# Two layers and a product-key expert block in fp32: the first two query panels of the second layer computed token tile by token tile, and the wait for the sub-keys moved

## The chip, the cores and the metric

The kernel runs on one core of a Trainium2 chip. The metric is the device time of one execution in microseconds (us), the median of three runs. Everything is computed to fp32 accuracy: each large product is three passes of TensorE over operands split in a high and a low part (high·high, high·low, low·high). All times of one instruction come from one profiled execution.

## The reference, cut to what matters

Two transformer blocks run one after the other on 256 tokens of width 1024. The second block has two layers (called layer 1 and layer 2 here, `l = 0` and `l = 1` in the code). Each layer is a mixing part, a layer norm, a product-key expert part, and another layer norm:

```python
y = jnp.concatenate([mix, mo], axis=-1) @ w_out[l]
x = _layer_norm(DN_ALPHA * x + y, ln_mix_g[l], ln_mix_b[l])
f = _peer(x, peer_w_q[l], peer_sub_keys[l], peer_u[l], peer_v[l])
x = _layer_norm(DN_ALPHA * x + f, ln_ffn_g[l], ln_ffn_b[l])

def _peer(x, w_q, sub_keys, u, v):
    xt = x.reshape(T, D)                                      # 256 x 1024
    q = (xt @ w_q).reshape(T, PEER_HEADS, 2, PEER_HALF)       # 8 heads, 2 sides, 128
    s = jnp.einsum('thpe,pne->thpn', q, sub_keys)             # 128 sub-keys for each side
    top_s, top_i = lax.top_k(s, PEER_TOPK)                    # 16 of each side
    ...                                                       # 16 of the 256 sums, softmax, experts
```

The change lies where `x` has just been normed and `q` is computed, in both layers.

## The kernel before, in words

**Weights.** All weights come as one stream of panels of 128 x 2048 fp32 (1 MB). SyncE loads panel `i` into `RAW[i % 4]`; ScalarE copies it rounded to `HI` (function `hi`, L467); VectorE, or GpSimd in a stretch of each layer, subtracts to get the low part `LO` (L982, L1577). There are four slots. TensorE waits for the low part (`lo_ready`) and counts used panels in `hp_used`; ScalarE may fill a `HI` slot again once the panel four earlier is used; SyncE may load a `RAW` slot again once its low part is made. The order on each engine is the order in which the Python code issues it; nothing is scheduled later.

**The norm.** The output product of the mixing ends in four PSUM banks: two token tiles of 128 tokens, two column halves. VectorE adds the residual (`add_mixed`, L1400), takes statistics, and norms one tile at a time (`norm_tile`, L1207 to L1216; the last step is L1215, which signals `x_tile`). TensorE then turns that tile, eight 128 x 128 transposes (`tile_transposes`, L1615) into `M[0]`, `M[1]` for tile 0 and `M[2]`, `M[3]` for tile 1; ScalarE copies out the high part `XH` (L487), VectorE the low part `XL` (L1005, signal `xl_ready`), each in two groups of four 128-column blocks. While tile 1 is normed, TensorE computes a panel of the memory keys in layer 1 (`mem_panel(3)`), and in layer 2 issues 20 products whose result is never read (`warm(20, M[2])`, L1597).

**The queries.** Eight panels follow from `w0` on, one for each head: `half(w0 + u, "cc")` computes 2 x 128 query columns for all 256 tokens, with the weight block stationary and the 256 turned tokens moving, 2 halves x 8 blocks x 3 passes = 48 matmuls (L1620 to L1622). ScalarE copies each result to `QP` (L827). `head_scores(h)` multiplies head `h` by the sub-keys `SK` (four fp32 matmuls, eight TensorE instructions, L2193), ScalarE copies the scores to `SC` (L816), and VectorE looks for the best 16 (`best16`, L1221 to L1231). The sub-keys come by a DMA that ScalarE issues after both tiles are normed, behind a store of `X` to DRAM (L819, L820). TensorE waits for `keys_loaded` ahead of the first query panel (L2196).

**Behind them.** From `d0 = w0 + 8` on come the dense expert panels. The first 32 are products alone, and in their course VectorE finishes the selection that started with the eight heads.

Of the kernel before, what the change touches and what calls it, by code (L numbers as in the profile page):

```python
# [12 lines left out]
ACT = mybir.ActivationFunctionType  # L13
AX = mybir.AxisListType

P = 128
LOW = 128
TOK = 256
TT = TOK // P
# [112 lines left out]
def build(nc, stream, x_in, mem_in, const_in, par_in, lb_in, par2_in, wg2_in, mask_in, lev_in, rows_in, sk_in, diag_in, out):  # L132
    ctx = ExitStack()
    with ctx:
        sems = {}

        def sem(name):
            if name not in sems:
                sems[name] = ctx.enter_context(nc.semaphore(name))
            return sems[name]  # L140
# [5 lines left out]
        def at(name, shape, dt=F32, off=None):  # L146
            size = int(np.prod(shape[1:])) * (2 if dt == BF16 else 4)
            o = cursor[0] if off is None else off
            if off is None:
                cursor[0] += (size + 63) // 64 * 64  # L150
            assert o + size <= end, (name, o + size, end)
            return nc.alloc_sbuf_tensor_at(name, list(shape), dt, offset=o)
# [78 lines left out]
        def cst(name):  # L231
            a, b = CONST[name]
            return CST[:, a:b]
# [5 lines left out]
        def flat(t):  # L239
            return t.rearrange("p a b -> p (a b)")  # L240
# [53 lines left out]
        topk0 = x0 + TABLE_AT * slot  # L294
        cursor[0] = topk0
        TFX = at("tfx", [P, 2, TT * PH, TOPK, TOPK], BF16, off=topk0)
        QP = at("qp", [P, 2 * PH, TOK])
        CD2 = at("cd2", [P, PH, CANDS], off=cursor[0])
        EQ = at("eq", [P, TT * PH, TOPK, TOPK], BF16, off=cursor[0] + 8192)
        SC = at("sc", [P, TT, 2 * PH, KEYS])  # L300
# [40 lines left out]
        PS = [ctx.enter_context(nc.psum_tensor(f"lin{i}", [P, 512], F32)) for i in range(4)]  # L341
        M = [ctx.enter_context(nc.psum_tensor(f"m{i}", [P, 512], F32)) for i in range(4)]
# [5 lines left out]
        bank_free = [sem(f"bank_free{i}") for i in range(4)]  # L348
# [13 lines left out]
        def evicted(eng, i, it=0):  # L362

            eng.wait_ge(bank_free[i % 4], reads_before(i) + 1 + it)
# [93 lines left out]
        def _(act):  # L458
# [63 lines left out]
            for l in range(DEPTH):  # L522
# [21 lines left out]
                for u in range(N_IN):  # L544
                    hi_to(h0 + u + 4)
                    i = h0 + u
# [7 lines left out]
                    if u == 4:  # L554
# [3 lines left out]
                        ins = act.activation(flat(VA[:]), b[:, 256:512], ACT.Copy)  # L558
# [68 lines left out]
            for l in range(DEPTH):  # L627
# [16 lines left out]
                else:  # L644
                    xh_tile(6, 1)
                    for u in range(N_SHARED):
                        hi_to(HP_SHARED + u + 4)
                        i = HP_SHARED + u
# [174 lines left out]
                for u in range(N_WQ):  # L823
                    hi_to(w0 + u + 4)
                    i = w0 + u
                    act.wait_ge(hp_used, i + 1)
                    act.activation(flat(QP[:, 2 * u:2 * u + 2, :]), PS[i % 4][:], ACT.Copy).then_inc(bank_free[i % 4], 1)  # L827
                    if u >= 1:
                        head_scores(u - 1)
                head_scores(PH - 1)  # L830
# [762 lines left out]
        def _(pe):  # L1593
            def warm(n, bank):

                for _ in range(n):
                    pe.matmul(bank[:, 0:256], cst("ident"), CST[:, 0:256], start=True, stop=True)  # L1597
# [12 lines left out]
            def tile_transposes(inst, tt):  # L1610

                pe.wait_ge(sem("x_tile"), 2 * (inst - 5) + tt + 1)
                for g in range(2):
                    for k in range(4):
                        ins = pe.transpose(M[2 * tt + g][:, P * k:P * k + P], X[:, tt, P * (4 * g + k):P * (4 * g + k) + P], cst("ident"))  # L1615
                    ins.then_inc(sem("t_done"), 1)
# [12 lines left out]
            def half(i, modes, it=0, hh=XH, hl=XL, k0=0, first=True, last=True, between=lambda c: None, inst=None, tiled=None):  # L1629

                hp_wait(i, it, first)

                def operand(start, k):

                    if inst is not None and start and k % 2 == 0:
                        pe.wait_ge(sem("xl_ready"), 4 * inst + k // 2 + 1)
                    if tiled is not None and start and k % 4 == 0:
                        pe.wait_ge(sem("xl_ready"), 4 * tiled + 2 + k // 4 + 1)

                s, b = i % SLOTS, PS[i % 4]  # L1640
                wh, wl = (t.rearrange("p (k n) -> p k n", k=KT) for t in (HI[s][:], low_part(i)))
                if modes == "rr":
                    for tt in range(TT):
                        if tt == 1:
                            between(0)
                        for k in range(KT):
                            operand(tt == 0, k)
                            ins = three(b[:, 256 * tt:256 * tt + 256], hh[:, k0 + k, P * tt:P * tt + P], hl[:, k0 + k, P * tt:P * tt + P],
                                        wh[:, k, :], wl[:, k, :], first and k == 0 and (last or tt == 0), last and k == KT - 1, skip_group_check=not (first and last))
                else:  # L1650
                    for c, mode in enumerate(modes):
                        if c == 1:
                            between(0)
                        n = slice(P * c, P * c + P)
                        if mode == "c":
                            for k in range(KT):
                                operand(c == 0, k)
                                ins = three(b[:, 256 * c:256 * c + 256], wh[:, k, n], wl[:, k, n], hh[:, k, :], hl[:, k, :], k == 0, k == KT - 1)
                        else:
                            for tt in range(TT):  # L1660
                                for k in range(KT):
                                    ins = three(b[:, 256 * c + P * tt:256 * c + P * tt + P], hh[:, k, P * tt:P * tt + P], hl[:, k, P * tt:P * tt + P],
                                                wh[:, k, n], wl[:, k, n], k == 0, k == KT - 1)
                ins.then_inc(hp_used, 1)
                between(1)
# [266 lines left out]
            for l in range(DEPTH):  # L1932
# [247 lines left out]
                if l == 0:  # L2180
                    mem_panel(3)
                else:
                    warm(20, M[2])
                tile_transposes(5 + 2 * l, 1)
                def head_scores(h):

                    evicted(pe, w0 + h)
                    if h >= 4:
                        pe.wait_ge(sem("keysc_ready"), PH * l + h - 3)
                    for tt in range(TT):  # L2190
                        for side in range(2):
                            c = 256 * tt + P * side
                            ins = pe.matmul(M[h % 4][:, c:c + P], QP[:, 2 * h + side, P * tt:P * tt + P], SK[:, side, :], start=True, stop=True)  # L2193
                    ins.then_inc(sem("keysc_done"), 1)

                pe.wait_ge(sem("keys_loaded"), 16 * (l + 1))  # L2196
                for u in range(N_WQ):
                    half(w0 + u, "cc", tiled=5 + 2 * l if u == 0 else None)
                    if u >= 1:
                        head_scores(u - 1)  # L2200
                head_scores(PH - 1)
                d0 = w0 + N_WQ
# [269 lines left out]
```

## Time and profile before

| what | value |
|---|---|
| median of 3 runs | 2642.83 us (2639.48 to 2645.89) |
| profiled execution, own time | 2644.11 us |
| its span in the trace | 2642.3 us |
| TensorE matmul busy | 2580.5 us, 98% of the span |
| VectorE, ScalarE, GpSimd busy | 64%, 50%, 6% |
| DMA | 520.14 MB, mean 197 GB/s |
| mean granted TensorE clock | 0.995 of full speed |

The execution's own time is 1.8 us longer than the span of its records. TensorE is busy nearly always, so what counts is where it stands still, where it does work that nobody needs, and where it runs at the lower of its two clocks. Such places are found in the list of waits, in the chain of work that ended last (each row is a start, a duration, and what was done) and in the windows.

### The profile page before, as it was taken

Reading aid. Unit: us, or ns where it says so; the run is one execution under the profiler, and the core shown is the slowest. Engines: PE = TensorE matmul, PEld = TensorE weight load, DVE = VectorE, ACT = ScalarE, POOL = GpSimd, SP = SyncE. Lnnn points to the kernel's source line nnn. Section 1 sums busy time; section 2 is a strip of 40 time slices with the busy share of each in tenths; the row PEclk is TensorE's granted clock in tenths of the full one; section 3 lists DMA queues with packets and bytes.
Section 4 is the critical chain, followed back from the end, with each engine's and each line's share of the span. In section 5 each row is a group of like instructions: output and inputs, shape, how many; then the busy total and the mean of one; then the engine's idle time right before and its main releaser. Section 6 shows DMA issues by size and latency. Waiting matters only on the chain.

```text
span 2642.3 us, 45690 instructions
## 1 busy us (share of the span) xinstructions
PE 2580.5 (98%) x18680; PEld 2352.4 (89%) x18680; DVE 1689.2 (64%) x2677; ACT 1323.8 (50%) x1585; POOL 163.1 (6%) x74
## 2 busy tenths in 40 slices
PE   8999999999999999999999999988999999999998
PEld 7889898798888999999999888978999999999887
DVE  5766457664456999655555666475999655555666
ACT  4455343454364679544444444443679544444443
POOL 0000000000003500000000000002600000000000
PEclk9999999999999999999999999999999999999999
DMA  6245552355526456766656675524456756666672
GB/s 244 94 180 190 193 211 94 135 203 196 195 90 219 145 203 228 287 217 212 221 210 222 231 275 183 205 80 152 154 195 236 285 210 222 214 215 217 230 273 106
DMA packets 75007, 520.14 MB, mean 197 GB/s; under 512 B 8352, under 2 KB 8624, under 8 KB 18928
## 3 DMA queue, kind: packets, MB, share of 16 engines
q1 hardware_dynamic: 58592, 424.70, 44.8%
q0 software_dynamic: 10208, 43.45, 4.7%
q10 hardware_dynamic: 6064, 49.97, 4.6%
q8 instruction: 103, 1.69, 0.3%
q14 instruction: 40, 0.33, 0.0%
HBM read 478.25 MB, written 39.85 MB: 196 GB/s over the span
## 4 chain that ended last, share of the span: by engine, by line
PE 88%; DVE 9%; ACT 2%; issue 1%; DMA 1%; ACTq 0%; DVEq 0%
PE lin L1620 17%; PE lin L1622 17%; PE lin L1621 17%; PE m L1620 9%; PE m L1621 9%; PE m L1622 9%; PE m L2214 4%; DVE lo L982 1%; PE m L1754 1%; PE lin L1816 1%; PE m L1597 1%; PE m L1775 1%; PE m L2193 0%; ACT hi L467 0%; PE m L2096 0%
## 5 line engine op out<-in xcount | busy, mean ns | idle before, releaser
L982 DVE TENSOR_TENSOR lo<-raw,hi 128x2048 fp32r<-128x2048 f32 x351 | 802.4, 2291 | 635.8 <-ACT hi L467 634.8
L467 ACT ACTIVATE hi<-raw 128x2048 fp32r<-128x2048 f32 x403 | 770.0, 1913 | 456.9 <-PE m L1622 331.7
L1620 PE MATMUL lin<-xh,hi 128*128 128x256 f32 x3376 | 954.4, 283 | 16.2 <-DMA sk<-keys 9.3
L1622 PE MATMUL lin<-xh,lo 128*128 128x256 f32 x3376 | 935.8, 277 | 0.0
L1621 PE MATMUL lin<-xl,hi 128*128 128x256 f32 x3376 | 935.8, 277 | 0.0
L1620 PEld LDWEIGHTS lin<-xh,hi 128*128 128x128 f32 x3376 | 636.4, 189 | 24.2 <-DMA sk<-keys 9.7
L1621 PEld LDWEIGHTS lin<-xl,hi 128*128 128x128 f32 x3376 | 636.6, 189 | 3.7 <-issue 1.0
L1622 PEld LDWEIGHTS lin<-xh,lo 128*128 128x128 f32 x3376 | 636.1, 188 | 0.0
L1620 PE MATMUL m<-hi,ah 128*128 128x512 f32 x1024 | 398.8, 389 | 0.0
L1621 PE MATMUL m<-lo,ah 128*128 128x512 f32 x1024 | 398.8, 389 | 0.0
L1622 PE MATMUL m<-hi,al 128*128 128x512 f32 x1024 | 398.6, 389 | 0.0
L841 ACT ACTIVATE h<-lin 128x512 f32<-128x512 f32 x128 | 76.2, 595 | 318.0 <-PE lin L1622 295.1
L1622 PEld LDWEIGHTS m<-hi,al 128*128 128x128 f32 x1024 | 192.2, 188 | 40.4
L1620 PEld LDWEIGHTS m<-hi,ah 128*128 128x128 f32 x1024 | 192.2, 188 | 38.3 <-DVE al L1493 0.8
L1621 PEld LDWEIGHTS m<-lo,ah 128*128 128x128 f32 x1024 | 192.2, 188 | 37.6
L1577 POOL TENSOR_TENSOR lo<-raw,hi 128x2048 fp32r<-128x2048 f32 x27 | 124.2, 4605 | 251.1 <-DVE lo L982 169.2
L2214 PE MATMUL m<-ob,oa 128*128 128x128 f32 x1024 | 135.2, 275 | 0.3 <-ACT ob L853 0.3
L2214 PEld LDWEIGHTS m<-ob,oa 128*128 128x128 f32 x1024 | 124.3, 191 | 1.5 <-issue 0.8
L1620 PE MATMUL lin<-hi,xh 128*128 128x256 f32 (+2 forms) x336 | 112.4, 334 | 4.7 <-DVE xl L997 2.0
L1583 POOL DMA_DIRECT2D g<-gate_table x32 | 28.3, 886 | 1328.3 <-DVE h L1488 971.8
L1621 PE MATMUL lin<-lo,xh 128*128 128x256 f32 (+2 forms) x336 | 109.6, 326 | 0.0
L1622 PE MATMUL lin<-hi,xl 128*128 128x256 f32 (+2 forms) x336 | 109.5, 326 | 0.0
(351 smaller groups left out, 2764.9 us busy)
## 6 DMA issues: line engine op xcount, KB each, us to landing
raw<-stream SPq DMA_DIRECT2D x403, 1024.0 KB, 4.8
gate_table<-stg ACTq DMA_DIRECT2D x16, 2048.0 KB, 10.9
g<-gate_table POOLq DMA_DIRECT2D x32, 1024.0 KB, 8.3
rows<-rows ACTq DMA_DIRECT2D x4, 1024.0 KB, 7.6
memh<-mem_turned_scratch POOLq DMA_DIRECT2D x3, 1024.0 KB, 5.0
meml<-mem_turned_scratch POOLq DMA_DIRECT2D x3, 1024.0 KB, 8.2
dg<-taps ACTq DMA_DIRECT2D x2, 1152.0 KB, 9.4
x_scratch<-x ACTq DMA_DIRECT2D x2, 1024.0 KB, 4.2
```

The costliest lines, as they stand in the source:

```text
L467: act.activation(HI[i % SLOTS][:], RAW[:, i % SLOTS, :], ACT.Copy).then_inc(hi_ready, 1)
L841: act.activation(H[:, s % AHEAD, :], PS[s % 4][:], ACT.Gelu).then_inc(sem("ge_ready"), 1)
L982: dve.tensor_tensor(low_part(i), RAW[:, i % SLOTS, :], HI[i % SLOTS][:].bitcast(F32), ALU.subtract).then_inc(lo_ready, 1)
L1577: pool.tensor_tensor(low_part(i), RAW[:, i % SLOTS, :], HI[i % SLOTS][:].bitcast(F32), ALU.subtract).then_inc(lo_ready, 1)
L1583: pool.dma_start(G[c % 2][:].rearrange("p g b t -> p g (b t)"), tab[l][:, :, GB * STORE * c:GB * STORE * c + GB * STORE].rearrange("g a x ...
L1597: pe.matmul(bank[:, 0:256], cst("ident"), CST[:, 0:256], start=True, stop=True)
L1620: pe.matmul(out_, ah, bh, start=first, stop=False, **kw)
L1621: pe.matmul(out_, ah, bl, start=False, stop=False, **kw)
L1622: return pe.matmul(out_, al, bh, start=False, stop=last, **kw)
L1754: last[j] = pe.matmul(to[:, 64 * tt:64 * tt + 64].rearrange("p (b m) -> p b m", m=m), KS[o, d, t], halves(QS[o, d, t], m)[:, :, 1 - d, :], ...
L1775: last[j] = pe.matmul(halves(M[3][o, c + P * tt:c + P * tt + P], m)[:, :, 1 - d, :], VR[:, tt, 64 * h:64 * h + 64], sc[:, 64 * tt:64 * tt ...
L2214: ins = pe.matmul(M[k % 4][:, KEYS * t:KEYS * t + KEYS], oa[:, t, :], ob[:, t, :], start=True, stop=True)
```

## The change

1. In layer 2 the 20 unread products are gone. In their place TensorE computes the tile 0 part of the query panels `w0` and `w0 + 1` (`row_half`, a function that was there already: the turned tokens are stationary, the 256 weight columns move, 24 matmuls for each tile of a panel). After the transposes of tile 1 come the tile 1 parts.
2. These two results stand token by column and not column by token, so ScalarE copies them to a new buffer `QTOK` (over the place of `QP[:, 0:4]`), TensorE turns them with eight transposes in the middle of panel `w0 + 2` (`queries_turned`), and ScalarE copies them to `QP`. The scores of head 0 and head 1 then both follow behind panel `w0 + 2`.
3. In both layers the wait for `keys_loaded` stands in `head_scores(0)` and no longer ahead of panel `w0`.

```diff
+        QTOK = at("qtok", [P, 2, TT, 256], off=topk0)
...
                 for u in range(N_WQ):
                     hi_to(w0 + u + 4)
                     i = w0 + u
+                    if l > 0 and u == 2:
+                        for j in range(2):
+                            act.wait_ge(sem("queries_turned"), j + 1)
+                            act.activation(flat(QP[:, 2 * j:2 * j + 2, :]), M[j][:], ACT.Copy).then_inc(sem("queries_ready"), 1)
                     act.wait_ge(hp_used, i + 1)
+                    if l > 0 and u < 2:
+                        act.activation(QTOK[:, u].rearrange("p t c -> p (t c)"), PS[i % 4][:], ACT.Copy).then_inc(bank_free[i % 4], 1)
+                        continue
                     act.activation(flat(QP[:, 2 * u:2 * u + 2, :]), PS[i % 4][:], ACT.Copy).then_inc(bank_free[i % 4], 1)
+                    if l > 0 and u == 2:
+                        head_scores(0)
                     if u >= 1:
                         head_scores(u - 1)
...
                 if l == 0:
                     mem_panel(3)
                 else:
-                    warm(20, M[2])
+                    row_half(w0, 5 + 2 * l, 0)
+                    row_half(w0 + 1, 5 + 2 * l, 0)
                 tile_transposes(5 + 2 * l, 1)
+                if l > 0:
+                    row_half(w0, 5 + 2 * l, 1)
+                    row_half(w0 + 1, 5 + 2 * l, 1)
+
+                def queries_turned(c):
+                    if c == 0:
+                        for u in range(2):
+                            evicted(pe, w0 + u)
+                            for side in range(2):
+                                for tt in range(TT):
+                                    ins = pe.transpose(M[u][:, 256 * side + P * tt:256 * side + P * tt + P],
+                                                       QTOK[:, u, tt, P * side:P * side + P], cst("ident"))
+                            ins.then_inc(sem("queries_turned"), 1)
+
                 def head_scores(h):
 
-                    evicted(pe, w0 + h)
+                    if h == 0:
+                        pe.wait_ge(sem("keys_loaded"), 16 * (l + 1))
+                    if l > 0 and h < 2:
+                        pe.wait_ge(sem("queries_ready"), h + 1)
+                    else:
+                        evicted(pe, w0 + h)
...
-                pe.wait_ge(sem("keys_loaded"), 16 * (l + 1))
                 for u in range(N_WQ):
-                    half(w0 + u, "cc", tiled=5 + 2 * l if u == 0 else None)
-                    if u >= 1:
+                    if l == 0:
+                        half(w0 + u, "cc", tiled=5 if u == 0 else None)
+                    elif u == 2:
+                        half(w0 + u, "cc", between=queries_turned)
+                        head_scores(0)
+                    elif u > 2:
+                        half(w0 + u, "cc")
+                    if u >= (1 if l == 0 else 2):
                         head_scores(u - 1)
```

On TensorE, at the norm of layer 2, before the change (`cst,x` are the transposes of a tile, `cst` alone the unread products, `lin` the query panel):

```order
7284 L1622 MATMUL lin<-hi_52,xl 128x512
7285 L1615 MATMUL m<-cst,x 128x128 x8
7286 L1597 MATMUL m<-cst 128x256 x20
7287 L1615 MATMUL m<-cst,x 128x128 x8
7288 L1620 MATMUL lin<-xh,hi_53 128x256
7289 L1621 MATMUL lin<-xl,hi_53 128x256
```

And with it, the same place (`hi_53` is panel `w0`, `hi_50` panel `w0 + 1`; lines 1615 to 1622 have become 1625 to 1632):

```order
7284 L1632 MATMUL lin<-hi_52,xl 128x512
7285 L1625 MATMUL m<-cst,x 128x128 x8
7286 L1630 MATMUL lin<-hi_53,xh 128x256
...
7310 L1630 MATMUL lin<-hi_50,xh 128x256
...
7334 L1625 MATMUL m<-cst,x 128x128 x8
7335 L1630 MATMUL lin<-hi_53,xh 128x256
...
7382 L1632 MATMUL lin<-hi_50,xl 128x256
7383 L1630 MATMUL lin<-xh,hi_51 128x256
...
7407 L2206 MATMUL m<-cst,qtok 128x128 x8
```

Between the two sets of transposes of `x` now stand 48 panel matmuls (7286 to 7333) in place of 20 unread ones; 48 more follow the second set, and panel `w0 + 2` (`hi_51`) comes right behind, with the eight transposes of the queries in its middle.

On ScalarE, at the same place, before the change (`qp` is the copy of the queries of a panel, `sc` that of the scores of a head):

```order
957 L487 ACTIVATE xh<-m 128x4x128 x2
958 L819 DMA x_scratch<-x 128x2048
959 L820 DMA sk<-keys 128x256
960 L827 ACTIVATE qp<-lin 128x512
961 L467 ACTIVATE hi_53<-raw 128x2048
962 L827 ACTIVATE qp<-lin 128x512
963 L816 ACTIVATE sc<-m 128x2x256
964 L467 ACTIVATE hi_50<-raw 128x2048
```

And with it:

```order
957 L488 ACTIVATE xh<-m 128x4x128 x2
958 L820 DMA x_scratch<-x 128x2048
959 L821 DMA sk<-keys 128x256
960 L833 ACTIVATE qtok<-lin 128x512
961 L468 ACTIVATE hi_53<-raw 128x2048
962 L833 ACTIVATE qtok<-lin 128x512
963 L468 ACTIVATE hi_50<-raw 128x2048
964 L830 ACTIVATE qp<-m 128x512 x2
965 L835 ACTIVATE qp<-lin 128x512
966 L817 ACTIVATE sc<-m 128x2x256 x2
```

ScalarE gains two copies (row 964) and now copies the scores of heads 0 and 1 together, behind the third panel.

## Rows read from the trace of the kernel before

**Rows 1.** The page: busy time of the engines (part 1); groups of instructions (part 5).
```profile
PE 2580.5 (98%) x18680; PEld 2352.4 (89%) x18680; DVE 1689.2 (64%) x2677; ACT 1323.8 (50%) x1585; POOL 163.1 (6%) x74
...
L467 ACT ACTIVATE hi<-raw 128x2048 fp32r<-128x2048 f32 x403 | 770.0, 1913 | 456.9 <-PE m L1622 331.7
L1620 PE MATMUL lin<-xh,hi 128*128 128x256 f32 x3376 | 954.4, 283 | 16.2 <-DMA sk<-keys 9.3
```

**Rows 2.** The chain that ended last, layer 2: start us, us, what.
```profile
1804.50 8.63 PE m L1597 x40
1813.14 0.45 PE m L1615 x4
...
1814.42 4.13 DMA sk<-keys
1818.60 0.58 PE lin L1620
...
1832.56 0.89 PE m L2193 x8
...
1838.92 0.89 PE m L2193 x8
```

**Rows 3.** Timeline of layer 2: start, us, engine, instruction [idle before, releaser].
```profile
1803.41 1.09 PE L1615 MATMUL m<-cst,x 128*128 128x128 f32 x8 [1.10 <-DVE x L1215]
...
1804.73 1.29 DVE L1005 TENSOR_TENSOR xl<-m,xh 128x512 fp32r<-128x512 f32 x2
...
1808.94 1.28 DVE L1215 SCALAR_TENSOR_TENSOR x<-x,small,rows 128x1024 f32<-128x1024 f32 x1
...
1814.10 0.59 ACT L487 ACTIVATE xh<-m 128x512 fp32r<-128x512 f32 x1
...
1814.31 1.29 DVE L1005 TENSOR_TENSOR xl<-m,xh 128x512 fp32r<-128x512 f32 x2 [4.08 <-ACT xh L487]
1815.52 2.28 DVE L982 TENSOR_TENSOR lo<-raw,hi 128x2048 fp32r<-128x2048 f32 x1
1817.88 4.55 POOL L1577 TENSOR_TENSOR lo<-raw,hi 128x2048 fp32r<-128x2048 f32 x1 [169.21 <-DVE lo L982]
```

**Rows 4.** The chain that ended last, layer 1.
```profile
823.29 4.21 DMA sk<-keys
827.55 0.38 PE lin L1620
...
840.35 0.89 PE m L2193 x8
```

**Rows 5.** Timeline of VectorE in layer 1.
```profile
823.18 1.29 DVE L1005 TENSOR_TENSOR xl<-m,xh 128x512 fp32r<-128x512 f32 x2 [1.45 <-ACT xh L487]
824.39 2.28 DVE L982 TENSOR_TENSOR lo<-raw,hi 128x2048 fp32r<-128x2048 f32 x1
```

**Rows 6.** Windows: stretch, us, busy by engine (count), granted clock, DMA share, GB/s.
```profile
763.10:769.90 6.80, 6.80 (x28) 5.95 (x28) 3.84 (x6) 5.00 (x10) 0.00 (x0) 0.50 0.44 154
1644.30:1651.10 6.80, 6.80 (x53) 6.55 (x54) 6.62 (x9) 3.30 (x5) 4.37 (x1) 1.00 0.16 40
...
827.90:831.30 3.40, 3.40 (x19) 3.40 (x18) 0.00 (x0) 0.00 (x0) 3.40 (x2) 0.50 0.88 308
1818.60:1824.60 6.00, 6.00 (x28) 6.00 (x29) 0.00 (x0) 0.00 (x0) 3.82 (x1) 0.50 0.63 199
```

**Rows 7.** Timeline of TensorE at two other waits.
```profile
759.73 0.28 PE L1620 MATMUL lin<-hi,xh 128*128 128x256 f32 x1
...
762.36 0.41 PE L2026 MATMUL m<-cst,pm 128*128 128x128 f32 x2 [2.12 <-DVE pm L1296]
...
1644.27 0.55 PE L1615 MATMUL m<-cst,x 128*128 128x128 f32 x3 [2.04 <-DVE x L1215]
```

**Rows 8.** The chain in the selection of layer 2: VectorE starts on two heads.
```profile
1872.31 0.89 DVE ts L1221 x4
...
1877.53 0.89 DVE ts L1221 x4
```

## The prediction, made before the changed kernel was run

> **What bounds the kernel now.** I began with the busy line of the page: TensorE's matmuls cover 98% of the span, every other engine has a third of it free or more [rows 1]. So a change is worth what it takes off TensorE's own path, and I looked for three things there: standing still, work nobody reads, and the lower clock. The groups of the page show the first: the query product's line stood idle 9.3 us for the sub-keys' DMA [rows 1]. The chain that ended last shows the rest. In layer 2, after the transposes of tile 0, TensorE spends 8.63 us on the 20 unread products (40 instructions), then turns tile 1, and then the chain leaves TensorE: the DMA of the sub-keys takes 4.13 us, and the first query matmul starts at 1818.60 [rows 2]. Layer 1 has the same wait, with a DMA of 4.21 us and the first matmul at 827.55 [rows 4]. The windows show the third: right behind both waits the granted clock is 0.50, the 1.2 GHz level of the two (1.2 and 2.4), for 6.0 us of matmuls in layer 2 and 3.4 us in layer 1 [rows 6].
>
> **Units.** A full query panel and the scores of a head: 1838.92 - 1832.56 = 6.36 us, of which the scores are 0.89, so the panel is 5.47 [rows 2]. From the first query matmul to the first scores stand two panels, 10.94 us at full clock. They took 1832.56 - 1818.60 = 13.96 in layer 2 and 840.35 - 827.55 = 12.80 in layer 1 [rows 2, 4]: 3.02 and 1.86 us lost to the lower clock.
>
> **Layer 1: only the wait moves.** What is late next is the low part of tile 1's tokens. VectorE makes its two groups from 823.18 in 1.29 us; the panel can start on the first group, at about 823.83 [rows 5]. So TensorE starts at 823.9 instead of 827.55: **3.65 us**. The low part of panel `w0 + 1` is made at 824.39 to 826.67 [rows 5] and needed at 823.9 + 5.5 = 829.4; no new wait. The keys, landed by 827.5 [rows 4], are needed at 834.8. The wait, 9.3 us in both layers together [rows 1], shrinks to about 1 us here; if the clock then holds, the **1.86 us** come too. Sum: 5.5 us.
>
> **Layer 2, step by step on TensorE.** The transposes of tile 0 end at 1804.50 [rows 2, 3].
> - The first group of tile 0's low part is ready at 1804.73 + 0.65 = 1805.38 [rows 3]. So TensorE stands still for about 0.9 us where the unread products were.
> - Two tile-0 parts, 48 matmuls. The trace has the row-wise form, 256 weight columns moving, at 0.28 us [rows 7], the page's mean for the other form being 0.283 [rows 1]. So I price a whole panel's worth at 5.47: end at 1810.9. Bounds: the same, or half the clock (10.9).
> - Tile 1 is normed at 1808.94 + 1.28 = 1810.22 [rows 3], before TensorE asks. That was also true of the unread products, which ran until 1813.14: they overshot by 2.9 us, and this much comes back whatever is put there.
> - Transposes of tile 1, ScalarE's copy, VectorE's subtraction: before, 1813.14 to 1814.31 + 0.65 = 1814.96, 1.82 us [rows 2, 3]. So tile 1's part can start at 1812.75. This path was there before, covered by the wait for the keys; now it stands bare, some 0.9 us of it idle.
> - Two tile-1 parts, 5.47: end at 1818.2. At this time the kernel before has not begun its first panel (1818.60).
> - Panel `w0 + 2`, 5.47, with eight transposes in its middle, priced like those of `x`, 0.9 to 1.1 us [rows 3]: end at 1824.7.
> - Scores of head 0 and 1, 1.78: end at 1826.5. Before, the second head's scores ended at 1839.81 [rows 2], with the same work done but for `w0 + 2`, which is then still to come; the kernel before has done panels `w0` to `w0 + 2` there as well (two panels, scores 0, a panel, scores 1). So the two points are the same place in the work: **13.3 us**.
> Check by difference: gone are 8.63 + 4.6 (wait) + 3.02 (clock) = 16.25; added are 0.9 + 0.9 idle and 1.0 of transposes, 2.8; net 13.4.
>
> **What hides the rest.** ScalarE copies `QTOK` twice in place of `QP`, same size. Between the end of the tile-1 parts (1818.2) and the scores (1824.7) it has the second copy (0.6), one `hi` (1.91 [rows 1]), and two copies of turned queries at 0.6 each [rows 3]: 3.7 us in 6.5, the last at about 1822.8. Gone that cover, each microsecond of lateness is one of TensorE's. The low part of `w0 + 2` is VectorE's behind tile 1 (2.28 us from 1815.52 before, from about 1813.5 now): ready 1815.8, needed 1818.2. `w0 + 3` is the first of GpSimd (4.55 us from 1817.88 before [rows 3], 1815.9 now): ready 1820.5, needed 1826.5; GpSimd's 4.55 a panel is below TensorE's 6.36. The keys are needed 8 us after they land. What is queued behind the moved wait on TensorE is `head_scores(0)` alone.
>
> **Does it last to the end?** VectorE needs 1877.53 - 1872.31 = 5.22 us for a head [rows 8]. Heads come from about 1826.3 on; eight in a row would end at 1868.1. The seventh is now ready at 1826.5 + 5 x 6.36 + 0.6 = 1858.9 and the eighth right behind it, so these two end at 1869.3, against 1877.53 + 5.22 = 1882.75 before. So VectorE is not the bound, by 1.2 us, and the selection behind it moves by the same 13.3. All that follows is started by semaphores relative to these, nothing by the time of day. I take nothing off.
>
> **The clock, weighed.** The one open price is the granted clock. Idle times of 1.10 us (before the transposes of tile 0, there already) and 0.9 behind them lie together in layer 2, without the unread products to cover the second. The trace has two waits of that sum: 2.12 us at 762.36, followed by 6.8 us at 0.50, and 2.04 us at 1644.27, followed by full clock [rows 6, 7]. One of two. So a fall costs half of 3.4 to 6.8 us, 1.7 to 3.4. The Trainium skill, "TensorE: Matmul & The Clock Gate", section "Part 1: The HAM clock gate (the 'warmup' mystery)", says that the slow clock is the default and that activity lifts it, and that the point of the switch varies from run to run. The two waits of the trace agree, and by this rule removing the unread products speaks against the change; its worst case is the third rival below.
>
> **Sum.** 5.5 + 13.35 = 18.9 us. Against the profiled execution, 2644.11 - 18.9 = 2625.2; the median of the runs is 1.3 lower, so **2624.0 us**.
>
> **Rivals.**
> 1. The clock falls once in one of the new idle places (two in layer 2, one in layer 1), or does not recover fully: 1.7 to 3.4 us, twice at most. For it: one of the two waits of that size. Against: both the falls I count as gone stand behind waits of 4.6 us. Time 2625.7 to 2631.
> 2. VectorE or ScalarE becomes the bound in layer 2. If a head took VectorE as long as TensorE's old cycle (6.36), eight from 1826.3 would end at 1877.2, and 7.8 us of 13.3 would be lost: 2632. Against: two heads stand back to back in the chain at 5.22 [rows 8]. Should the moved wait do nothing in layer 1, because the panel waits there for something no row shows, 5.5 us are lost: 2629.5.
> 3. Slower. The unread products are what holds TensorE's clock in layer 2, and without them it stays at 1.2 GHz through the query part. That part is 8 x 5.47 + 8 x 0.89 + 2 = 53 us at full clock and would last 53 longer: 2642.8 - 18.9 + 53 = 2677. It decides against the change once the lower clock lasts over 38 us in all, since half of that is the gain. Against: the low stretches here last 3.4 to 6.8 us, under continuous matmuls [rows 6].
> 4. The change does not do what it says, the parts by token being held until tile 1 is there. Then layer 2 loses the overlap of 5.5 us and keeps the rest: 2629.5. Against: `row_half` waits for the groups of its own tile alone, and the order on TensorE has it ahead of tile 1's transposes.
>
> **Chances.** Forecast as it stands 0.60; rival 1 0.24; rival 2 and 4 together 0.10; no change in the end, gain given back behind the selection, 0.04; rival 3 0.02. A measurement of this kernel tells about 0.2%, 5.3 us, from no change. The first three are all faster by more than that, but I leave some of them, and of what I have not seen, for a smaller gain: faster 0.92, same 0.05, slower 0.03. Range: runs of one kernel spread by 3 us either side, so from 2619 (forecast, with one of the other low stretches of the run gone as well) to 2631 (the clock falls twice).
>
> **What would show it.** No wait of TensorE for the sub-keys. In layer 1 head 0's scores 11 us behind the first low group of tile 1, not 840.35 - 823.83 = 16.5. In layer 2 two idle places of about 0.9 us, a granted clock of 1.00 around them, and from the end of tile 0's transposes to the end of head 1's scores 22 us instead of 35.3. Wrong would be: a clock of 0.50 there, a wait of the scores for ScalarE, a wait of `w0 + 2` for its low part, or VectorE without idle time between the heads and the selection ending late against TensorE's dense panels.

## The result, and the profile after

| | before | changed |
|---|---|---|
| median | 2643.65 us (4 runs, 2639.48 to 2645.89) | 2624.42 us (4 runs, 2622.61 to 2624.61) |
| profiled execution, span | 2642.3 us | 2622.8 us |
| ratio, 95% interval | | 0.9925 [0.9913, 0.9938] |

The change takes 19.2 us off the medians, 16.4 to 23.0 by the interval. 2624.0 was forecast.

The page of the changed kernel answers to [rows 1]: TensorE is as busy as before, in a shorter span, and the idle time ahead of the query product's line has halved.

```profile
PE 2567.4 (98%) x18648; PEld 2341.1 (89%) x18648; DVE 1689.8 (64%) x2677; ACT 1324.9 (51%) x1587; POOL 163.0 (6%) x74
...
L1630 PE MATMUL lin<-xh,hi 128*128 128x256 f32 x3344 | 943.4, 282 | 8.1 <-DVE lo L992 4.6
```

Layer 2, TensorE's timeline of the changed kernel (start us, us, engine, instruction, idle time before it and releaser). It answers to [rows 3]:

```profile
1796.52 1.09 PE L1625 MATMUL m<-cst,x 128*128 128x128 f32 x8 [1.11 <-DVE x L1225]
1798.68 0.36 PE L1630 MATMUL lin<-hi,xh 128*128 128x256 f32 x1 [1.07 <-DVE xl L1015]
...
1799.11 0.28 PE L1630 MATMUL lin<-hi,xh 128*128 128x256 f32 x1
...
1804.05 0.28 PE L1630 MATMUL lin<-hi,xh 128*128 128x256 f32 x1
...
1806.49 0.38 PE L1630 MATMUL lin<-hi,xh 128*128 128x256 f32 x1 [1.05 <-DVE xl L1015]
```

The chain that ended last in the same place, which answers to [rows 2]: it no longer leaves TensorE for a DMA, only for the copy and the subtraction behind tile 1's transposes.

```profile
1804.57 0.45 PE m L1625 x4
1805.04 0.61 ACT xh L488
1805.74 0.70 DVE xl L1015
1806.49 0.38 PE lin L1630
...
1815.15 0.87 PE m L2206 x8
...
1818.78 1.78 PE m L2223 x16
```

What is to be seen: two idle places of 1.07 and 1.05 us where the 20 unread products and the wait for the keys were, the eight transposes of the queries at 0.87 us, and the scores of heads 0 and 1 in one piece, ending at 1818.78 + 1.78 = 1820.56. The windows over the tile 0 parts and over the tile 1 parts (stretch, us, busy by engine and count, granted clock, DMA share, GB/s) have the full clock:

```profile
1798.70:1804.50 5.80, 5.80 (x49) 5.80 (x50) 4.49 (x6) 2.32 (x3) 0.00 (x0) 1.00 0.01 3
1806.50:1812.30 5.80, 5.80 (x49) 5.80 (x50) 2.73 (x2) 2.40 (x2) 2.99 (x1) 1.00 0.77 274
```

The same chain in layer 1 answers to [rows 4]:

```profile
818.34 0.67 PE m L1625 x4
...
819.73 0.70 DVE xl L1015
820.43 0.14 issue
820.57 0.36 PE lin L1630
...
831.73 0.89 PE m L2223 x8
```

**Where the time went, by two stretches.** Totals move by some microseconds from run to run, so I measure two stretches of the trace, each from a fixed instruction to a fixed instruction. *Stretch 1* (layer 1) runs from the first transpose of tile 1 to the first product of head 0's scores: the chain before has 821.79 and 840.35, 18.56 us; now 818.34 to 831.73, 13.39 us. *Stretch 2* (layer 2) runs from the first transpose of tile 0 to the end of head 1's scores: before 1803.41 to 1838.92 + 0.89, 36.40 us; now 1796.52 to 1820.56, 24.04 us. The gains are 5.17 and 12.36, together 17.5 us. The two spans differ by 19.5. The other 2.0 us come mostly from the clock in places that the change did not touch: the windows have it at 0.50 there, and at other places in the two executions. Before, besides the 6.8 us from 763.10 [rows 6]:

```profile
483.20:486.60 3.40, 3.40 (x9) 2.61 (x9) 3.26 (x5) 0.00 (x0) 0.00 (x0) 0.50 0.00 0
1636.20:1639.60 3.40, 3.40 (x17) 2.81 (x16) 3.37 (x4) 0.00 (x0) 0.00 (x0) 1.00 0.49 166
```

And changed:

```profile
483.20:486.60 3.40, 3.40 (x17) 2.83 (x15) 3.30 (x4) 0.03 (x1) 0.00 (x0) 1.00 0.00 0
762.40:765.80 3.40, 3.40 (x18) 3.40 (x18) 3.30 (x6) 3.37 (x10) 0.00 (x0) 0.50 0.40 169
...
1636.20:1639.60 3.40, 3.40 (x12) 2.86 (x11) 3.19 (x6) 2.99 (x3) 3.40 (x1) 0.50 0.00 0
```

A stretch of 3.4 us at half the clock loses half of it, 1.7 us. Ahead of stretch 1 the changed kernel has two of them fewer (one at 483, and 3.4 in place of 6.8 us at 763) and was already 821.79 - 818.34 = 3.45 us early. Between the stretches it has one more (at 1636) and lost 1.73 of that (1803.41 - 1796.52 = 6.89, against 3.45 + 5.17). The rest, 0.3 us, lies behind stretch 2.

### The profile page after: what moved, and what is told of

It is laid out like the page before. It is cut to its first block, busy times and chain, and to the rows that moved or that the text cites. A ratio compares the mean times of both kernels' runs of the same rounds, so it can differ in the third digit from the quotient of the medians.

```text
span 2622.8 us, 45628 instructions
## 1 busy us (share of the span) xinstructions
PE 2567.4 (98%) x18648; PEld 2341.1 (89%) x18648; DVE 1689.8 (64%) x2677; ACT 1324.9 (51%) x1587; POOL 163.0 (6%) x74
## 4 chain that ended last, share of the span: by engine, by line
PE 88%; DVE 9%; ACT 1%; issue 1%; DMA 0%; ACTq 0%; DVEq 0%
PE lin L1630 17%; PE lin L1632 17%; PE lin L1631 17%; PE m L1631 9%; PE m L1630 9%; PE m L1632 9%; PE m L2249 4%; DVE lo L992 1%; PE m L1764 1%; PE lin L1826 1%; PE m L1785 1%; PE m L2223 0%; ACT hi L468 0%; PE m L2106 0%; PE m L1797 0%
## 5 line engine op out<-in xcount | busy, mean ns | idle before, releaser
L1630 PE MATMUL lin<-xh,hi 128*128 128x256 f32 x3344 | 943.4, 282 | 8.1 <-DVE lo L992 4.6
L1631 PE MATMUL lin<-xl,hi 128*128 128x256 f32 x3344 | 925.0, 277 | 0.0
L1632 PE MATMUL lin<-xh,lo 128*128 128x256 f32 x3344 | 924.9, 277 | 0.0
L1630 PEld LDWEIGHTS lin<-xh,hi 128*128 128x128 f32 x3344 | 628.1, 188 | 15.8 <-issue 6.8
L1631 PEld LDWEIGHTS lin<-xl,hi 128*128 128x128 f32 x3344 | 628.5, 188 | 3.7 <-issue 1.0
L1632 PEld LDWEIGHTS lin<-xh,lo 128*128 128x128 f32 x3344 | 628.0, 188 | 0.0
L1630 PE MATMUL lin<-hi,xh 128*128 128x256 f32 (+2 forms) x368 | 121.0, 329 | 6.8 <-DVE xl L1015 2.1
L1632 PE MATMUL lin<-hi,xl 128*128 128x256 f32 (+2 forms) x368 | 117.8, 320 | 0.0
L1631 PE MATMUL lin<-lo,xh 128*128 128x256 f32 (+2 forms) x368 | 117.4, 319 | 0.0
```

What stands on the lines that cost most here:

```text
L1630: pe.matmul(out_, ah, bh, start=first, stop=False, **kw)
L1631: pe.matmul(out_, ah, bl, start=False, stop=False, **kw)
L1632: return pe.matmul(out_, al, bh, start=False, stop=last, **kw)
```

## The experiments

All of them change the kernel before or the changed kernel; `before` stands for a median of its runs on the same chip. Stretches as above, from the one trace of each kernel.

| kernel | median us (runs) | ratio to before, 95% | stretch 1 | stretch 2 |
|---|---|---|---|---|
| before | 2643 to 2644 | | 18.56 | 36.40 |
| changed | 2624.42 (4) | 0.9925 [0.9913, 0.9938] | 13.39 | 24.04 |
| e1, wait moved only | 2632.79 (5) | 0.9961 [0.9947, 0.9975] | 13.39 | 30.12 |
| e2, by token only | 2631.80 (5) | 0.9963 [0.9949, 0.9977] | 19.80 | 24.04 |
| e3, e1 without unread products | 2630.80 (5) | 0.9964 [0.9950, 0.9978] | 13.38 | 29.88 |
| e4, e1 with 12 of the 20 | 2631.23 (4) | 0.9956 [0.9939, 0.9972] | 13.36 | 27.51 |
| e5, idle place filled | 2623.39 (5) | 0.9927 [0.9914, 0.9941] | 13.39 | 23.09 |
| e6, column form | 2657.13 (10) | 1.0037 [1.0022, 1.0053] | | 53.59 |
| e8, queries turned twice | 2625.09 (1) | | | 24.92 |
| e9, e11, row form elsewhere | 2625.85, 2628.64 (1 each) | | | |
| e10, e5 with low parts in line | 2627.09 (5) | 0.9933 [0.9920, 0.9947] | | 23.08 |

**e1: the moved wait alone.**

```diff
 def head_scores(h):
+    if h == 0:
+        pe.wait_ge(sem("keys_loaded"), 16 * (l + 1))
     evicted(pe, w0 + h)
...
-                pe.wait_ge(sem("keys_loaded"), 16 * (l + 1))
```

> The kernel before with the wait for the sub-keys moved and nothing else. My theory (three sources that add: the wait with its low clock, the unread products that overshoot, the covered latencies): layer 1 as in the changed kernel, 5.2 us; layer 2 the first query matmul 3.6 us earlier and 3.0 us of low clock gone, 6.6. In all 11.8 us under the kernel before, about 2632. Rival (the whole gain is the moved wait, the panels by token merely refill the time of the unread products): as fast as the changed kernel, about 2624.

Stretch 1 is that of the changed kernel; stretch 2 is 36.40 - 30.12 = 6.28 us shorter (6.6 expected). TensorE's timeline in layer 2 shows that the first query panel now waits 1.14 us for the low part of the tokens, and the window behind it is at full clock (see [rows 2] and [rows 6] for what stood there):

```profile
1810.24 1.04 PE L1615 MATMUL m<-cst,x 128*128 128x128 f32 x8
1812.41 0.36 PE L1620 MATMUL lin<-xh,hi 128*128 128x256 f32 x1 [1.14 <-DVE xl L1005]
```

```profile
1812.00:1818.00 6.00, 5.59 (x49) 5.62 (x50) 3.06 (x3) 0.00 (x0) 2.86 (x1) 1.00 0.80 280
```

The moved wait is worth 5.17 + 6.28 = 11.5 us in both layers; the rival that it is everything is out, by 6 us of stretch 2 and by the medians.

**e2: the panels by token alone**, the wait back ahead of the loop over the panels.

```diff
 def head_scores(h):
-    if h == 0:
-        pe.wait_ge(sem("keys_loaded"), 16 * (l + 1))
...
+                pe.wait_ge(sem("keys_loaded"), 16 * (l + 1))
                 for u in range(N_WQ):
```

> The changed kernel with the wait for the sub-keys back at its old line, ahead of the loop over the query panels. In layer 2 that is now behind both parts of two panels, at about 1812, when the keys have been there for 2 us, so nothing should be waited for there. Layer 1 waits 4.6 us again and falls to the lower clock. My theory: 5.2 us above the changed kernel, about 2629.6. Rival (the moved wait is the whole gain in layer 2 as well): about 2636 or more.

Stretch 2 stays at 24.04: in layer 2 the old line of the wait costs nothing any more. Stretch 1 is 19.80, above the 18.56 of before, since the low clock lasted longer this time. TensorE waits only once, for 4.67 us, and then runs at 0.50; timeline and window of layer 1:

```profile
824.21 0.58 PE L1630 MATMUL lin<-xh,hi 128*128 128x256 f32 x1 [4.67 <-DMA sk<-keys]
```

```profile
823.60:830.30 6.70, 6.09 (x28) 6.09 (x29) 0.00 (x0) 0.00 (x0) 6.70 (x2) 0.50 0.70 234
```

The traces say that the moved line matters in layer 1 alone once the panels are computed by token, and without that in both.

**e3: nothing in place of the unread products** (e1 without `warm(20, M[2])`).

```diff
                 if l == 0:
                     mem_panel(3)
-                else:
-                    warm(20, M[2])
```

> As e1_wait_only, and the 20 unread products of layer 2 are gone with nothing in their place. TensorE idles from about 1804.5 to 1810.2 and turns tile 1 some 2.9 us earlier than in e1. If the granted clock holds, 2629. If the unread products are what holds it (third rival of the prediction), 0.50 for 3.4 to 6.8 us of the query panels, 1.7 to 3.4 us back: 2630.7 to 2632.4, no better than e1. Were the clock low all through the query part, 2680.

TensorE stands still for 5.78 us, then for 0.72, and what it gains by turning tile 1 earlier it pays back at the lower clock. Timeline and windows:

```profile
1802.83 1.97 PE L1615 MATMUL m<-cst,x 128*128 128x128 f32 x8 [5.78 <-DVE x L1215]
1805.52 0.55 PE L1620 MATMUL lin<-xh,hi 128*128 128x256 f32 x1 [0.72 <-DVE xl L1005]
```

```profile
1802.90:1809.50 6.60, 5.88 (x26) 5.51 (x27) 3.58 (x3) 1.19 (x2) 1.06 (x1) 0.50 0.54 186
1809.60:1815.60 6.00, 6.00 (x55) 6.00 (x54) 0.00 (x0) 2.40 (x2) 3.43 (x1) 1.00 0.61 228
```

Stretch 2 is 29.88 against 30.12 in e1: the unread products did hold the clock, and dropping them is worth 0.2 us. Real products in their place hold it as well, as the changed kernel shows.

**e4: 12 unread products in place of 20** (e1 with `warm(12, M[2])`).

> As e1_wait_only with 12 unread products in place of 20: 12 x 0.43 = 5.2 us, ending at about 1809.7, just ahead of tile 1's norm at 1810.2. My theory: the overshoot of 2.9 us comes back and the clock holds, 2629. The rest to the changed kernel, about 4.5 us, is then what computing real panels in that time is worth. Rival (the clock depends on how long the unread products run): 0.50 behind them, 2631 or more.

They end just ahead of tile 1, TensorE waits 0.60 us, and the clock stays (1.00 from 1809.4 to 1815.4):

```profile
1801.19 5.34 PE L1597 MATMUL m<-cst 128*128 128x256 f32 x24
1807.13 1.09 PE L1615 MATMUL m<-cst,x 128*128 128x128 f32 x8 [0.60 <-DVE x L1215]
1809.36 0.35 PE L1620 MATMUL lin<-xh,hi 128*128 128x256 f32 x1 [1.14 <-DVE xl L1005]
```

Stretch 2 is 27.51, 2.6 us under e1: the overshoot of the unread products, 2.9 in the prediction. From here to the changed kernel it is another 3.5 us of stretch 2; that is what real work in this time is worth, once its transposes, its second idle place and its slower pace are paid (4.5 expected). The median lies only 1.6 us under e1's, with overlapping ranges (2628.18 to 2632.12 and 2630.56 to 2635.46), so this step rests on the traces.

**e5: the second idle place filled.** The last 3 of 8 blocks of the tile 0 part of `w0 + 1` go behind the transposes of tile 1.

```diff
                     row_half(w0, 5 + 2 * l, 0)
-                    row_half(w0 + 1, 5 + 2 * l, 0)
+                    row_half(w0 + 1, 5 + 2 * l, 0, (0, 5))
                 tile_transposes(5 + 2 * l, 1)
                 if l > 0:
+                    row_half(w0 + 1, 5 + 2 * l, 0, (5, KT))
                     row_half(w0, 5 + 2 * l, 1)
```

> The changed kernel, but the last 3 of 8 blocks of the tile 0 part of panel w0 + 1 (9 matmuls, 9 x 0.118 = 1.06 us) stand behind the transposes of tile 1 in place of ahead of them. Tile 1 is normed at 1803.3 there and TensorE reaches its transposes at 1804.45, so they can start 1.1 us earlier, and the 9 matmuls fill the 1.04 us in which TensorE waits for tile 1's low part. My theory (the covered latency now stands bare, and only there): from the first transpose of tile 0 to the end of head 1's scores 23.0 us in place of 24.04, total 1.0 us less, about 2623.4. Rival (VectorE's chain is as late as TensorE): no change.

The idle place is gone (TensorE's timeline; the nine matmuls run from 1806.51, the tile 1 part starts at 1807.80 with no wait in front of it):

```profile
1805.66 1.09 PE L1625 MATMUL m<-cst,x 128*128 128x128 f32 x8
1806.51 0.36 PE L1630 MATMUL lin<-hi,xh 128*128 128x256 f32 x1
...
1807.80 0.39 PE L1630 MATMUL lin<-hi,xh 128*128 128x256 f32 x1
```

Stretch 2 is 23.09, 0.95 us less. To compare the totals, both kernels ran once more in turn:

> The changed kernel once more, on the same chip and in turn with e13, so that the two can be compared: 18.7 us under the kernel before by the prediction, 17.5 by the two stretches of the traces.

> The kernel of e5_gap_filled once more, beside e12. The traces give it 0.95 us less than the changed kernel in the stretch, 0.04% of the run; my theory: its median lies about 1 us under that of e12, with spreads of 2 to 5 us, so the sign may not be told by totals. Rival: the 9 moved matmuls cost something elsewhere and the median lies above.

The changed kernel had a median of 2626.96 us (5 runs, 2624.10 to 2628.15), the filled one 2626.30 (5 runs, 2623.28 to 2627.19); ratios to before 0.9937 [0.9923, 0.9950] and 0.9932 [0.9918, 0.9945]. The traces of these two give 24.09 and 23.08 us for stretch 2, so the gain of about 1 us is shown in two pairs of traces; in the totals the sign agrees both times, and the size is below what they tell.

**e6: the column form.** `row_half` replaced by a function with the weight block stationary and 128 tokens moving; transposes of the queries and their copies dropped, the token buffer no longer used.

```diff
-                    row_half(w0, 5 + 2 * l, 0)
+                    column_tile(w0, 5 + 2 * l, 0)
...
+                for c in range(2):
+                    for k in range(KT):
+                        ins = three(PS[i % 4][:, 256 * c + P * tt:256 * c + P * tt + P], wh[:, k, n], wl[:, k, n],
+                                    XH[:, k, P * tt:P * tt + P], XL[:, k, P * tt:P * tt + P], k == 0, k == KT - 1)
```

> The changed kernel with the two panels by token in the other form: weight block stationary, 128 turned tokens moving, twice the matmuls (48 a part) of half the columns. The result stands column by token, so the token buffer, the eight transposes and two copies are gone. Rival view (the row form and its turning is overhead): saves 0.9 us of transposes, 2623.5. Theory from the trace: 16 such matmuls of 128 columns in the first block start 0.112 us apart, no closer than those of 256, so a part costs 5.4 us in place of 2.8, four parts 10.3 more, less 0.9: the stretch 33.4 us in place of 24.04, total about 2633.8.

Slower than the kernel before by the median, and 20 us beyond my own estimate for stretch 2. The first matmuls start 0.11 us apart, as expected: half the columns, the same pace. But from 1807.12 on each takes 0.42 us and they start 0.21 apart. Timeline, then windows:

```profile
1805.09 0.30 PE L1623 MATMUL lin<-xh,hi 128*128 128x128 f32 x1 [1.07 <-DVE xl L1008]
...
1807.01 0.27 PE L1625 MATMUL lin<-xh,lo 128*128 128x128 f32 x1
1807.12 0.35 PE L1623 MATMUL lin<-xh,hi 128*128 128x128 f32 x1
...
1807.49 0.42 PE L1625 MATMUL lin<-xh,lo 128*128 128x128 f32 x1
1807.70 0.41 PE L1623 MATMUL lin<-xh,hi 128*128 128x128 f32 x1
```

```profile
1804.90:1807.10 2.20, 2.01 (x18) 2.04 (x19) 2.13 (x5) 0.00 (x0) 0.00 (x0) 1.00 0.03 7
1807.20:1823.60 16.40, 16.40 (x79) 16.40 (x78) 2.52 (x2) 2.26 (x3) 0.00 (x0) 0.50 0.00 0
...
1846.00:1851.50 5.50, 5.50 (x27) 5.50 (x27) 0.00 (x0) 2.39 (x2) 1.99 (x1) 0.50 0.36 153
1852.00:1855.00 3.00, 3.00 (x28) 3.00 (x28) 0.00 (x0) 0.22 (x1) 2.10 (x1) 1.00 0.00 0
```

The granted clock is 0.50 (1.2 GHz) through all four parts, though TensorE was busy for 16.40 of 16.40 us, and it is back only in the panel behind, whose matmuls have 256 columns: that panel starts at 1846.81 and runs at 0.50 until about 1851.4. Three of the ten runs took 2643.36, 2643.87 and 2646.42 us, the other seven 2655.5 to 2660.86. The mean granted clock on record is 0.993 to 0.994 in the three and 0.987 to 0.990 in the seven, so the clock was low for less time in the three. Where it was low there is not shown, since only one of the seven was profiled. Either way the row form with its turning is the cheaper one.

**e8: the queries turned twice** (`for side in (0, 1, 0, 1)`), one run.

> The changed kernel with the eight transposes of the queries done twice. Theory: they lie bare on TensorE and nothing waits for them: the stretch grows by 0.9 us, 24.04 to 24.95. Rival (the scores of head 0 wait for ScalarE's copies, which the trace shows ending 2.1 us ahead of the next thing ScalarE does): growth of more than 0.9, with an idle place of TensorE ahead of the scores.

Stretch 2 grows from 24.04 to 24.92 us, by 0.88. The transposes lie bare on TensorE, and ScalarE's copies of the turned queries are covered: in this run ScalarE had them done and then idled 2.16 us until panel `w0 + 2` was finished, whose result it copies next.

```profile
1819.29 0.60 ACT L835 ACTIVATE qp<-lin 128x512 f32<-128x512 f32 x1 [2.16 <-PE lin L1632]
```

**e9, e10, e11: why the parts by token run at 0.118 us a matmul.** (e9 and e11 compute later panels in row form and leave out the turning of their queries; only their pace counts.) In the changed kernel 42 of them lie between 1799.11 and 1804.05, 0.1176 us each; a column-form panel has 5.47 / 48 = 0.114 with its start. At 96 matmuls the gap is 0.4 us.

> The changed kernel with panels w0 + 3 and w0 + 4 of layer 2 in row form too, where the column form ran at 0.113 us a matmul; their queries are not turned, so the scores of heads 3 and 4 are of other numbers. The panels by token ran at 0.118. If the form sets the price: 0.118 here, panels of 5.66 us in place of 5.44. If the place sets it (what went before, or what the other engines do): 0.113 here. The matmuls of the same form at about 728 in the trace start 0.113 apart, which speaks for the place.

> As e5_gap_filled, and the low parts of panels w0 and w0 + 1 of layer 2 lie at the same offset in their slots as the high parts, as those of several other row-form panels do; before they lay 128 bytes further. If the offset makes the row form's 0.118 us a matmul, it is 0.113 here: 96 x 0.0045 = 0.43 us less than e5, stretch 22.6 us in place of 23.0. If not, as e5. The row-form panels of the shared keys at 1639 lie in line and ran at 0.118, which speaks against the offset.

> As the changed kernel, but in layer 2 panel w0 + 4 is computed in row form directly behind the column form of panel w0 + 3, the scores of head 2 coming behind both (in e9 those scores, in plain fp32, stood between). Its queries are not turned, so head 4's scores are of other numbers. If what ran before sets the pace of the row form (column form before: 0.113, as at 727 in the trace; fp32 products or transposes before: 0.118, as in e9 and in the panels by token), it is 0.113 here. If the form alone sets it, 0.118.

In e9, the matmuls of `w0 + 3` and `w0 + 4` in row form start 0.118 apart (18 of them from 1829.91 to 1832.04), in a place where column form has 0.113. In e10 the other offset of the low part gives stretch 2 of 23.08 against 23.09: no effect. In e11, directly behind a column panel, it is 0.118 too (the first two lines are the end of the column panel, the others the row panel; 9 matmuls in 1830.74 - 1829.68 = 1.06):

```profile
1829.57 0.28 PE L1634 MATMUL lin<-xh,lo 128*128 128x256 f32 x1
1829.68 0.28 PE L1632 MATMUL lin<-hi,xh 128*128 128x256 f32 x1
...
1830.74 0.28 PE L1632 MATMUL lin<-hi,xh 128*128 128x256 f32 x1
```

Both of my explanations by place fell. The form goes with 0.118 wherever these runs put it, but in the first panels of that form in layer 1 the changed kernel's trace has 0.113 (six matmuls in 728.47 - 727.79 = 0.68 us):

```profile
727.79 0.28 PE L1630 MATMUL lin<-hi,xh 128*128 128x256 f32 x1
...
728.47 0.28 PE L1630 MATMUL lin<-hi,xh 128*128 128x256 f32 x1
```

What tells the two apart stays open.

## Why the prediction was right, point by point

- **Layer 1: 3.65 + 1.86 us.** Measured 5.17 against 5.5: the first query matmul comes 5.76 - 2.23 = 3.53 us earlier against the start of the stretch, and 1.64 us follow. The panel waits 1.14 us for the low part and runs at full clock (1.00 from 820.6 to 831.7); the keys are needed long after they land. The missing 0.3 us are in the start: the first matmul came 0.14 us behind the low part and took 0.36 itself.
- **Layer 2: 13.35 us.** Measured 12.36. From the end of tile 0's transposes the steps were priced at 0.9 idle, 5.47, 1.85, 5.47, 5.47 + 1.0, 1.78. They took 1.07, 5.89 (1798.68 to 1804.57), 1.92 (to 1806.49), 12.29 for the next three together (to 1818.78; 11.94 priced), and 1.78. The mis-sized term is the price of the parts by token. The tile 0 parts cost 0.42 us more than the 5.47 I took for them, and the tile 1 parts about as much again, since the transposes of the queries, 0.87, were cheaper than priced. Half of each 0.42 is pace: I took the column form's 5.47 because single matmuls had the same duration, 0.28 us [rows 7], but a duration is not a pace, and 48 steps of 0.118 in place of 0.113 or 0.114 are 0.2 us more. The other half is the start: behind an idle place the first matmul counts 0.36 us in the chain and not 0.12, which the sum put at nothing. The pace stood in the trace of before. It has six such parts, three panels of the shared keys by two tiles, two behind the transposes at 1644.27 [rows 7] and four behind those at 1652.16. In its timeline 36 matmuls of them take 1657.98 - 1653.74 = 4.24 us, 0.118 each. The prediction did not read them:

```profile
1653.74 0.28 PE L1620 MATMUL lin<-hi,xh 128*128 128x256 f32 x1
...
1657.98 0.28 PE L1620 MATMUL lin<-hi,xh 128*128 128x256 f32 x1
```

  With the idle place 0.2 us longer this makes the 1.0.
- **The clock.** 1.00 in stretch 2, as in the likeliest case. Idle times of 0.9 to 1.1 us did not bring it down in any of the nine traces of kernels with the row form there (changed, e2, e5, e8 to e13). That it would hold was not certain. The prediction weighed two single waits of about 2 us, and overlooked the place of the trace of before that is nearest in shape, two idle places of 1.04 and 0.81 us with 1.13 us of work between them:

```profile
480.97 1.13 PE L1825 MATMUL m<-ac,cst 128*128 128x256 f32 x4 [1.04 <-DVE ac L1155]
482.91 0.60 PE L1620 MATMUL lin<-hi,xh 128*128 128x512 f32 x1 [0.81 <-DVE xl L1136]
```

  The clock was 0.50 right behind it (483.20 in the windows above). All fourteen traces have this pair, and five of them the fall (before, e4, e6, e10, e13).
- **The unread products.** The prediction split their cost in an overshoot of 2.9 us and the use of the rest. e4 gives 2.6 for the first, e4 to the changed kernel 3.5 for the second.
- **Third rival.** Its condition, that the clock depends on what fills the time, is real (e3, e6). Its premise, that query work would not hold the clock, is wrong in the row form; with 128 moving columns (e6) it came true for 44 us.
- **Fourth and second rival.** The parts by token did run ahead of tile 1. VectorE idled 11.1 us until the first scores, then took the first heads back to back, starting at 1820.34 and 1825.55, 5.21 us each. The seventh starts at 1853.07, having waited 1.18 us for ScalarE's copy of the scores. Before it started at 1872.31 [rows 8], so the selection moved by 19.2 us, what TensorE had gained up to there (6.89 + 12.36).
- **The sum.** 18.9 forecast, 17.5 in the two stretches, 19.2 in the medians. That the median hit 2624.0 within 0.4 us is partly luck: the 1.3 us of over-estimate were made up by low-clock stretches elsewhere, which shift totals by some microseconds in either direction. The five later runs of the same kernel (e12) had a median of 2626.96 us, 16.7 under that of before.

## What to carry to other kernels

Where an engine is kept busy with unread work to hold its clock, ask first for how long (2.6 us of the 8.6 were pure delay here), then for work whose inputs are already there: half the tokens are normed 7 us ahead of the others. A wait for a small DMA belongs ahead of its first reader, not ahead of the loop; here it cost 3.5 us of its 4.6, and another 1.6 (layer 1) to 2.8 us (layer 2, by e1) behind it, most of that in clock. Price a moved product by the distance of its starts in the form that it will have, add the start behind an idle place, and look in the trace for a place that has that form already.

## What the runs showed of the hardware that I had not expected

- **The clock fell under nearly unbroken work.** With matmuls of 128 columns, back to back at 0.111 us, the granted clock went to 0.50 after 2.1 us and stayed there for 44 us, to 1851.4. The trace has no idle place in that time but 0.6 us ahead of tile 1's part, long after the fall. The idle places just ahead of the first of these matmuls, 0.92 and 1.07 us, are about those of the changed kernel, and the row form has no fall behind them in nine traces. So the two forms differ in what the clock did, though e6 has one trace only. The Trainium skill, "TensorE: Matmul & The Clock Gate", section "HAM oscillation — how this bites in real kernels", warns of idle gaps; e6 has the long low stretch with nearly none in it.
- **Half the moving columns did not make a matmul cheaper.** At full clock the starts lie 0.111 us apart with 128 moving columns (e6) and 0.113 with 256. The Trainium skill, "TensorE: Matmul & The Clock Gate", section "LDWEIGHTS (loading the stationary operand)", says that a weight load takes its time by the columns of the stationary operand. The trace agrees, as both have 128 of these; that the weight loads set the pace is argued, since no run changed them alone.
- **Waits of about 2 us brought the clock down in one execution and not in another.** An idle time of 5.78 us, and one of 0.72 behind it, brought about 10 us at 0.50 (e3, 1799.4 to 1809.5 by the windows, the idle time included). Those of about 1 us in the two stretches brought none. Between them the same place went either way: the wait of 2.04 us at 1644.27 was followed by the full clock before [rows 6, 7], and that of 2.05 us at the same place of the changed kernel by 3.4 us at 0.50 (1636.20 in the windows). The pair at 481 (above) was followed by 0.50 in five traces and by the full clock in nine.

```profile
1635.64 1.49 PE L1625 MATMUL m<-cst,x 128*128 128x128 f32 x8 [2.05 <-DVE x L1225]
```

- **One form, two paces.** In the changed kernel's trace row-form products of equal shape started 0.113 us apart at 728 and 0.118 everywhere in the query part. Neither the offset of the low part (e10) nor what ran before (e11) is the reason.
